# Attention scores of two mixers: full-precision products against three one-pass products of high and low parts

## The chip, the core and the metric

One core of one Trainium2 chip runs the whole kernel. The metric is device microseconds (us) of one execution. The engines meant below are TensorE (PE; PEld is its weight load), VectorE (DVE), ScalarE (ACT), GpSimd (POOL) and SyncE (SP), which only issues transfers.

## The reference

Two decoder layers over 512 tokens of width 2048. Layer 0 mixes an S5 state-space branch, eight forgetting-attention heads (FoX) and four memory heads. Layer 1 mixes eight latent-attention heads (MLA), eight sparse-attention heads (NSA, two key groups of four heads each) and four memory heads. The part that matters is the scores:

```
# FoX, per head: q, k (512, 128)
s = q @ k.T * scale + cum[:, None] - cum[None, :]        # causal, then softmax
# NSA, per head: three score sets from one q
s_c = q @ kc.T * scale + bias      # compressed keys, 31 of them (padded to 32)
s_s = q @ ks.T * scale + bias      # selected blocks; all of them here, so plain causal
s_w = q @ kw.T * scale + bias      # window of 512, causal here
o = g0 * softmax(s_c) @ vc + g1 * softmax(s_s) @ vs + g2 * softmax(s_w) @ vw
```

## The kernel before, in words

Every large product is made from split operands: a float32 value x is written as a high part (x rounded to the type float32r) and a low part (x minus the high part), and a product is the sum of three matmuls, high*high, high*low and low*high. The scores of FoX and NSA are not made so: their operands are plain float32, one matmul each, which the trace shows as two LDWEIGHTS and two MATMUL records.

The heads run in two sequences, `SEQ0` (FoX and memory heads of layer 0) and `SEQ1` (NSA and memory heads of layer 1). A sequence is a list of units, one unit being a score block of 128 query rows against `w` keys. For FoX a head has four units with `w` = 512, 128, 384, 256 (`ORDER` = 3, 0, 2, 1). For NSA a head has twelve: for each query block i, a unit of the selected keys, one of the window keys, both with `w` = (i+1)*128, and one of the 32 compressed keys; where i < 3 the first takes the compressed keys along in one matmul (`w` + 32 columns). `pe_seq` is written out by hand: step x makes the scores of unit x, the transposes of unit x-3 (L2609), the values of unit x-4 (L2620), and between them a slice of a large output projection, the fill (L283). DVE takes the maximum (L2702), ACT the exponential (L2664), DVE normalises (L2716, L2718), ACT copies the transposes out (L2656).

`pool_seq` on GpSimd issues the loads of the heads from its own queue, in program order: for head H it waits until the values of head H-2 are done and loads `v(H)`, then waits for the scores of head H-1 and loads q and k of head H+1 (`qk(H+1)`), then the gate of head H. For `SEQ1` the loads `qk(0)` are issued early, then GpSimd waits for the last MLA head (`MLA.fin`), and goes on with `v(0)`, `qk(1)`, `gate(0)`. A head's first score waits on the semaphore `a_ld` of its q and k loads, its first values on `a_vld`:

```python
if u["k"] == 0:
    pe.wait_ge(a_ld[u["r"]], t.ld0[0] + u["ld"])
```

Of the kernel before, what the change touches and what calls it, by code (L numbers as in the profile page):

```python
# [16 lines left out]
F32 = mybir.dt.float32  # L17
# [41 lines left out]
def build(nc, a):  # L59
    x, mem = a["x"][0], a["mem"][0]  # L60
    out = a["out"][0]
    with ExitStack() as ctx:
# [43 lines left out]
        bank_done = sem("bank_done")  # L106
        stored = sem("stored")
        ident_ok = sem("ident_ok")
        mask_ok = sem("mask_ok")
        gains_in = sem("gains_in")  # L110
        gains_pe, gains_ok = sem("gains_pe"), sem("gains_ok")
# [2621 lines left out]
        def pool_seq(pool, t, early=0):  # L2733

            def qk(H):
                if H >= 2:
                    pool.wait_ge(a_sc, t.u0 + t.end[H - 2])
                    if t.units[t.start[H - 2]]["bias"] is not None:
                        pool.wait_ge(a_mx, t.u0 + t.end[H - 2])
                t.units[t.start[H]]["load_qk"](pool, a_ld[H % 2])  # L2740

            def v(H):
                if H >= 2:
                    pool.wait_ge(a_pv, t.u0 + t.end[H - 2])
                t.units[t.start[H]]["load_v"](pool, a_vld[H % 2])

            def gate(H):
                if H >= 2:
                    pool.wait_ge(a_fin0, t.h0 + H - 1)
                pool.dma_start(t.units[t.start[H]]["out_gate"], t.units[t.start[H]]["gate_rows"]).then_inc(a_gl[H % 2], 16)  # L2750

            if early == 1:
                qk(0)
                return
            n = len(t.start)
            for H in range(n):
                if H == 0 and early == 0:
                    qk(0)
                if H == 0 and n > 1:
                    v(0)  # L2760
                    qk(1)
                    gate(0)
                    continue
                v(H)
                if H + 1 < n:
                    qk(H + 1)
                gate(H)

        resid_in = sem("resid_in")
        seqV = [s_tile(1024 * r, 2).rearrange("p (s j d) -> p s j d", s=2, j=4) for r in range(2)]  # L2770
# [5 lines left out]
        def head_units(H, units, **head):  # L2776
# [4 lines left out]
                out_.append(dict(u, H=H, r=H % 2, k=k, ld=ld, vld=vld, vn=head["vn"], **{n: head[n] for n in ("out_gate", "gate_rows", "load_qk", "load_v")}))  # L2781
            return out_

        def fox_head(h):

            r = h % 2
# [2 lines left out]
            def score(i):  # L2789
                def run(pe, bank):  # L2790
                    w = (i + 1) * P
                    nc.tensor.matmul(bank[:, 0:w], q[:, i * P:i * P + P], k[:, 0:w], start=True, stop=False)
                    return causal_mask(bank, w)
                return run

            def load_qk(pool, s_):
                qk = S[:, 8192 + 1536 * r:9216 + 1536 * r].rearrange("p (s t) -> p s t", s=2)
                pool.dma_start(qk, yE[2048:4096, :].rearrange("(s r) t -> r s t", s=2)[h * P:(h + 1) * P, :, :]).then_inc(s_, 16)
                pool.dma_start(cumB[r], cumD[h:h + 1, :].broadcast_to([P, T])).then_inc(s_, 16)

# [495 lines left out]
        def mla_score(i):  # L3296
            def score(pe, bank, r, b, x):
                w = (i + 1) * P
                q, k = MLA.inp[r][0], MLA.inp[r][1]
                nc.tensor.matmul(bank[:, 0:w], q[:, i * P:i * P + P], k[:, 0:w], start=True, stop=False)  # L3300
                if x % 4 == 0:
                    pe.wait_ge(rot_low, num(b, 2, x // 4 + 2 - 2 * MLA.b0))
                for part in range(2):
                    nc.tensor.matmul(bank[:, 0:w], rotQ[r][:, i * P:i * P + P], rotK[part][:, 0:w], start=False, stop=False)  # L3304
                causal_mask(bank, w).then_inc(MLA.sc, 1)
# [5 lines left out]
        qrS, krS = s_tile(10240), s_tile(11264)  # L3311

        rotQ, rotK = [A[:, 8 + e, :] for e in range(2)], [A[:, 10 + part, :] for part in range(2)]
        rot_high, rot_low = sem("rot_high"), sem("rot_low")

        def act_rot_keys(act):
            act.wait_ge(rope_ok, 2)
            nc.scalar.activation(rotK[0], krS, ACT.Copy).then_inc(rot_high, 1)

        def dve_rot_keys(dve):  # L3320
            dve.wait_ge(rot_high, 1)
            nc.vector.tensor_tensor(rotK[1], krS, rotK[0].bitcast(F32), ALU.subtract).then_inc(rot_low, 1)

        def act_rot(act, h):
# [7 lines left out]
        def dve_rot(dve, h):  # L3332

            half, other = [slice(64 * e, 64 * e + 64) for e in (h % 2, 1 - h % 2)]
            dve.wait_ge(rot_high, h + 2)
            nc.vector.tensor_tensor(rotQ[h % 2][other, :], qrS[half, :], rotQ[h % 2][half, :].bitcast(F32), ALU.subtract).then_inc(rot_low, 1)

        def rot_at(t, b, x):
# [58 lines left out]
        def pool_sum(pool, dst, e, h=0):  # L3397
            half = slice(64 * e, 64 * e + 64)
            if h >= 2:
                pool.wait_ge(rot_low, h)  # L3400
            nc.gpsimd.tensor_tensor(dst[half, :], qa[half, :], qb[half, :], ALU.add).then_inc(rope_ok, 1)

        def pool_rotary_load(pool, h):
# [19 lines left out]

        a_tiles = lambda k, n: A[:, k:k + n, :].rearrange("p k t -> p (k t)").bitcast(F32)
        nsaK0 = A[:, 16:20, :].rearrange("p k t -> p (k t)").bitcast(F32)
        nsaQ, nsaKw = [[nsaK0[:, o:o + 512], S[:, 8192 + o1:8704 + o1]] for o, o1 in ((0, 0), (1024 + NPAD, 512))]
        nsaKcs = [nsaK0[:, 512:1024 + NPAD], S[:, 10240:10752 + NPAD]]
        nsaKc, nsaKs = [[k[:, o:o + n] for k in nsaKcs] for o, n in ((0, NPAD), (NPAD, 512))]
        nsaB = [a_tiles(36, 3)[:, 0:LB], S[:, 13312:13312 + LB]]
        nsaVc = [a_tiles(39, 1)[:, 128:256], S[:, 15136:15264]]  # L3430
        nsaG = [S[:, 7680:8192], S[:, 9728:10240]]
# [1 line left out]
        def nsa_head(h):  # L3433

            r, grp = h % 2, h // 4
            keys = (nsaKs[r], nsaKw[r], nsaKc[r])

            def score(i, which, w):
                q = nsaQ[r][:, i * P:i * P + P]
                if i == 3:  # L3440
                    return lambda pe, bank: nc.tensor.matmul(bank[:, 0:w], q, keys[which][:, 0:w], start=True, stop=True)  # L3441
                if which == 0:
                    return lambda pe, bank: nc.tensor.matmul(bank[:, 0:NPAD + w], q, nsaKcs[r][:, 0:NPAD + w], start=True, stop=True)  # L3443
                if which == 1:
                    return lambda pe, bank: nc.tensor.matmul(bank[:, 0:w], q, nsaKw[r][:, 0:w], start=True, stop=True)  # L3445
                return None

            def load_qk(pool, s_):
                pool.dma_start(nsaQ[r], yO[1024 + h * P:1152 + h * P, :]).then_inc(s_, 16)
                for k in range(2):  # L3450
                    pool.dma_start((nsaKs, nsaKw)[k][r], yO[2560 + 256 * k + grp * P:2688 + 256 * k + grp * P, :]).then_inc(s_, 16)
                pool.dma_start(nsaB[r], biasD[:, h, :]).then_inc(s_, 16)
                if h == 0:
                    pool.wait_ge(cmp_out, 32)
                pool.dma_start(nsaKc[r], cmpD[grp, :, 0:NPAD]).then_inc(s_, 16)

            def load_v(pool, s_):
                pool.dma_start(nsaVc[r], cmpD[grp, :, NPAD:]).then_inc(s_, 16)
# [4 lines left out]
            for i in ORDER:  # L3463
                w = (i + 1) * P
                for which in (0, 1, 2):
# [4 lines left out]
                                      at=NPAD if which == 0 and i < 3 else 0,  # L3470
                                      v=(lambda j_, k=which: seqV[r][:, k, j_, :] if k < 2 else nsaVc[r]), bias=nsaB[r][:, o:o + n],
                                      gate=gtmS[:, i, col:col + 1], first=which == 0, last=which == 2))
            return head_units(h, units, ld=80 * (h // 2 + 1), vld=48 * (h // 2 + 1), vn=3, out_gate=nsaG[r],
                              gate_rows=yO[5120 + h * P:5248 + h * P, :], load_qk=load_qk, load_v=load_v)

        SEQ1 = Seq(1, [u for h in range(8) for u in nsa_head(h)] + [u for h in range(4) for u in mem_head(1, h, yO, 3584, 6144, 320, 192)], OUT1A, h1D, 1)

        def pe_nsa_gates(pe):
            pe.wait_ge(rope_in, 128)
# [467 lines left out]
```

## Time and profile before

| | us |
|---|---|
| median of 3 runs (lowest, highest) | 2172.55 (2171.39, 2172.58) |
| the profiled execution, its own time | 2172.06 |
| span of the profiled execution, first to last instruction | 2170.3 |

The rows further down are of the profiled execution. Times in them count from the span's first instruction. MATMUL records overlap: the duration of one holds its latency, so a spacing is read from start to start.

### The profile page before, as it was taken

The numbers are of one execution on the slowest core, as the hardware profiler recorded it, in microseconds if no ns is written. First come the engines' busy times: TensorE is split into PE (matmuls) and PEld (weight loads), VectorE is DVE, ScalarE is ACT, GpSimd is POOL, SyncE is SP. The second block draws the span as 40 slices with busy tenths as digits, with TensorE's granted clock in tenths as the row PEclk, the third lists the DMA queues.
The fourth block names the chain that finished last, engine by engine and source line by source line (L and its number), as shares of the span: only waits on it lengthen the run. The fifth ranks groups of instructions, "written<-read, shape, count | busy, mean of one in ns | idle before, by whom it ended". The sixth has DMA issues, their size and how long they took to land. (4 is left out here: it accounts for less than half of the span.)

```text
span 2170.3 us, 32485 instructions
## 1 busy us (share of the span) xinstructions
PE 2151.5 (99%) x12292; PEld 1810.8 (83%) x12292; DVE 1350.6 (62%) x2244; ACT 920.8 (42%) x1558; POOL 579.5 (27%) x771
## 2 busy tenths in 40 slices
PE   9999999999999999999999999999999999999998
PEld 8988888888888878888888899899886778788887
DVE  6632456655542237568649778877776648666876
ACT  6432333333332434434444444444433455555443
POOL 2626122223221002112001444444311255221120
PEclk9999999999999999999999999999999999999999
DMA  8645444444445436648644886878747966554674
GB/s 311 205 140 137 125 130 130 118 128 135 137 123 186 128 99 203 222 148 212 175 156 120 203 202 162 202 185 193 176 152 237 293 216 198 173 193 145 226 164 146
DMA packets 222423, 376.19 MB, mean 173 GB/s; under 512 B 22623, under 2 KB 102191, under 8 KB 220099
## 3 DMA queue, kind: packets, MB, share of 16 engines
q1 hardware_dynamic: 125152, 185.36, 27.8%
q0 software_dynamic: 63152, 126.20, 24.2%
q10 hardware_dynamic: 33971, 62.63, 7.9%
q8 instruction: 95, 1.56, 0.3%
q14 instruction: 53, 0.43, 0.1%
HBM read 310.30 MB, written 63.83 MB: 172 GB/s over the span
## 5 line engine op out<-in xcount | busy, mean ns | idle before, releaser
L283 PE MATMUL PS<-A,wsp 128*128 128x512 f32 (+2 forms) x3156 | 693.8, 379 | 2.9 <-issue 1.7
L283 PEld LDWEIGHTS PS<-A,wsp 128*128 128x128 f32 (+1 forms) x3156 | 564.2, 188 | 119.0 <-issue 9.1
L250 DVE TENSOR_TENSOR wsp<-wraw,wsp 128x1024 fp32r<-128x1024 f32 (+1 forms) x295 | 356.5, 1212 | 468.6 <-ACT wsp L243 467.0
L283 PE MATMUL PS<-wsp,A 128*128 128x512 f32 x2352 | 616.2, 403 | 0.0
L243 ACT ACTIVATE wsp<-wraw 128x1024 fp32r<-128x1024 f32 (+1 forms) x295 | 304.9, 1039 | 509.6 <-PE PS L283 406.7
L283 PEld LDWEIGHTS PS<-wsp,A 128*128 128x128 f32 x2352 | 423.8, 189 | 77.5 <-issue 4.8
L2044 PE MATMUL PS<-A,wsp 128*128 128x512 f32 x640 | 222.6, 397 | 0.0
L2046 PE MATMUL PS<-A,wsp 128*128 128x256 f32 x640 | 166.4, 280 | 0.0
L2001 DVE TENSOR_TENSOR wsp<-wraw,wsp 128x1024 fp32r<-128x1024 f32 x80 | 111.3, 1394 | 39.3 <-ACT wsp L1983 39.1
L2044 PEld LDWEIGHTS PS<-A,wsp 128*128 128x128 f32 x640 | 116.2, 188 | 21.8
L2046 PEld LDWEIGHTS PS<-A,wsp 128*128 128x128 f32 x640 | 120.7, 189 | 6.2
L1983 ACT ACTIVATE wsp<-wraw 128x1024 fp32r<-128x1024 f32 x80 | 84.8, 1060 | 95.0 <-PE PS L2046 49.0
L2656 ACT ACTIVATE S<-PS 128x256 f32<-128x256 f32 (+3 forms) x160 | 63.0, 394 | 131.8 <-PE PS L2609 131.0
L2057 PEld LDWEIGHTS PS<-S_rounded,wsp 128*128 128x128 f32 x960 | 117.8, 188 | 1.0
L2057 PE MATMUL PS<-S_rounded,wsp 128*128 128x256 f32 x960 | 118.3, 282 | 0.0
L1682 PE MATMUL PS<-wsp,A 128*128 128x512 f32 x504 | 114.9, 389 | 0.1
L1682 PEld LDWEIGHTS PS<-wsp,A 128*128 128x128 f32 x504 | 94.5, 188 | 20.1 <-DVE wsp L250 0.6
L1843 POOL TENSOR_TENSOR S<-wraw 128x1024 f32<-128x1024 f32 x20 | 59.3, 2967 | 189.3 <-DVE wsp L2001 76.7
L1983 ACT ACTIVATE wsp<-S 128x1024 fp32r<-128x1024 f32 x60 | 63.7, 1061 | 97.2 <-PE PS L2057 69.0
L2620 PEld LDWEIGHTS PS<-S 128*128 128x128 f32 x640 | 93.1, 191 | 9.4
L2001 DVE TENSOR_TENSOR wsp<-S,wsp 128x1024 fp32r<-128x1024 f32 x60 | 85.3, 1422 | 23.8 <-ACT wsp L1983 23.5
L2664 ACT ACTIVATE S<-PS,stats 128x256 f32<-128x256 f32 (+3 forms) x160 | 74.8, 467 | 51.4 <-DVE stats L2702 42.5
(455 smaller groups left out, 2841.4 us busy)
## 6 DMA issues: line engine op xcount, KB each, us to landing
wraw<-in_even_w_in_dram SPq DMA_DIRECT2D x112, 512.0 KB, 3.7
wraw<-in_odd_w_in_dram SPq DMA_DIRECT2D x96, 512.0 KB, 4.7
wraw<-in_w_out_dram SPq DMA_DIRECT2D x74, 512.0 KB, 4.6
wraw<-in_mem_w_kv_dram SPq DMA_DIRECT2D x32, 512.0 KB, 4.8
wraw<-in_w_out_dram POOLq DMA_DIRECT2D x24, 512.0 KB, 6.5
yO<-stage ACTq DMA_DIRECT2D x12, 1024.0 KB
yE<-stage ACTq DMA_DIRECT2D x10, 1024.0 KB
wraw<-in_odd_w_in_dram POOLq DMA_DIRECT2D x20, 512.0 KB, 8.8
```

What stands on the lines that cost most here:

```text
L243: nc.scalar.activation(wsp[:, q, 0, :, 0:j["cols"]], wraw[:, q, :, 0:j["cols"]], ACT.Copy).then_inc(w_hi, 1)
L250: nc.vector.tensor_tensor(wsp[:, q, 1, :, 0:j["cols"]], wraw[:, q, :, 0:j["cols"]], wsp[:, q, 0, :, 0:j["cols"]].bitcast(F32), ALU.subtrac ...
L283: mm = nc.tensor.matmul(dst, lhs, rhs, start=(s == 0 and kk == 0 and i == 0), stop=(s == j["spc"] - 1 and kk == 1 and i == 2))
L1682: mm = nc.tensor.matmul(PS[:, PAIR_BANK[product] + f, :], x_tile(j, product, 2 * s + kk, low)[:, f * P:f * P + P], wsp[:, q, wp, kk, :], s ...
L1983: nc.scalar.activation(fast_split(n % RAW, 0), fast_raw(FAST_RAW[product], s), ACT.Copy).then_inc(w_hi, 1)
L2001: nc.vector.tensor_tensor(fast_split(n % RAW, 1), fast_raw(FAST_RAW[product], s), fast_split(n % RAW, 0).bitcast(F32), ALU.subtract).then_ ...
L2044: mm = nc.tensor.matmul(dst, fast_split(q, 0)[:, w], fast_moving_both(product, 4 * s + kt), start=first, stop=last)
L2046: mm = nc.tensor.matmul(dst[:, 0:256], fast_split(q, 1)[:, w], fast_moving(product, 4 * s + kt, False), start=False, stop=False)
L2057: mm = nc.tensor.matmul(dst[:, f, :], w, fast_moving(product, 4 * s + kt, low), start=(s == 0 and f == 0 and m == 0), stop=(s == 1 and f = ...
L2620: mm = nc.tensor.matmul(PS[:, 7, i * P:i * P + P], u["v"](j_), seqT[x % 2][:, j_ * P:j_ * P + P], start=(j_ == 0 and u["first"]), stop=(j_ ...
L2656: nc.scalar.activation(seqT[x % 2][:, 0:n], PS[:, 6, 0:n], ACT.Copy).then_inc(a_ev, 1)
L2664: nc.scalar.activation(seqP[c][:, 0:w], PS[:, 4 + x % 2, u["at"]:u["at"] + w], ACT.Exp, bias=stats[:, 4 + c:5 + c], scale=-1.0 if u["bias" ...
```

## The change

For FoX and NSA the operands q and k are split into a high and a low part on GpSimd (`pool_split`: a copy to the high tile, a wait on GpSimd's own semaphore, and a subtraction in place that leaves the low part in the loaded tile). Each score matmul becomes three matmuls on float32r tiles. The split of head H+1 stands in GpSimd's program behind `gate(H)`; the split of NSA head 0 (both key tiles and q) stands behind `qk(0)`, ahead of the wait for `MLA.fin`; the keys of the second NSA group are split behind the split of head 3. A head's first score now also waits on `rot_low`. NSA keys are loaded once per group (with heads 0 and 2) instead of once per head. The semaphores `rot_high` and `rot_low`, which MLA uses, are shared, so MLA's counts are raised by a constant.

```diff
@@ -106,6 +106,8 @@
         bank_done = sem("bank_done")
         stored = sem("stored")
         ident_ok = sem("ident_ok")
+        rot_high, rot_low = sem("operand_high"), sem("operand_low")
+        FOX_SPLITS = 16
         mask_ok = sem("mask_ok")
         gains_in = sem("gains_in")
         gains_pe, gains_ok = sem("gains_pe"), sem("gains_ok")
...
@@ -2751,6 +2753,7 @@
             if early == 1:
                 qk(0)
+                pool_nsa_split(pool, 0)
                 return
             n = len(t.start)
             for H in range(n):
...
@@ -2760,11 +2763,18 @@
                     v(0)
                     qk(1)
                     gate(0)
+                    if t.l:
+                        pool_nsa_split(pool, 1)
+                    else:
+                        pool_fox_split(pool, 0)
+                        pool_fox_split(pool, 1)
                     continue
                 v(H)
                 if H + 1 < n:
                     qk(H + 1)
                 gate(H)
+                if H + 1 < 8:
+                    (pool_nsa_split if t.l else pool_fox_split)(pool, H + 1)
         resid_in = sem("resid_in")
         seqV = [s_tile(1024 * r, 2).rearrange("p (s j d) -> p s j d", s=2, j=4) for r in range(2)]
...
@@ -2781,6 +2791,19 @@
                 out_.append(dict(u, H=H, r=H % 2, k=k, ld=ld, vld=vld, vn=head["vn"], **{n: head[n] for n in ("out_gate", "gate_rows", "load_qk", "load_v")}))
             return out_
+        foxH = [[A[:, 16 + 2 * r + i, :] for i in range(2)] for r in range(2)]
+        def fox_operands(h):
+            o = 8192 + 1536 * (h % 2)
+            return [(S_rounded[:, o + 512 * i:o + 512 * i + 512], foxH[h % 2][i]) for i in range(2)]
+        def pool_fox_split(pool, h):
+            pool.wait_ge(a_ld[h % 2], 32 * (h // 2 + 1))
+            if h == 0:
+                pool.wait_ge(slot_used, E2["slot0"] + 1)
+            pool_split(pool, fox_operands(h), 2 * h)
         def fox_head(h):
             r = h % 2
...
@@ -2789,12 +2812,18 @@
             def score(i):
                 def run(pe, bank):
                     w = (i + 1) * P
-                    nc.tensor.matmul(bank[:, 0:w], q[:, i * P:i * P + P], k[:, 0:w], start=True, stop=False)
+                    (q_low, q_high), (k_low, k_high) = fox_operands(h)
+                    rows = slice(i * P, i * P + P)
+                    if i == ORDER[0]:
+                        pe.wait_ge(rot_low, 2 * h + 2)
+                    nc.tensor.matmul(bank[:, 0:w], q_high[:, rows], k_high[:, 0:w], start=True, stop=False)
+                    nc.tensor.matmul(bank[:, 0:w], q_low[:, rows], k_high[:, 0:w], start=False, stop=False)
+                    nc.tensor.matmul(bank[:, 0:w], q_high[:, rows], k_low[:, 0:w], start=False, stop=False)
                     return causal_mask(bank, w)
                 return run
             def load_qk(pool, s_):
-                qk = S[:, 8192 + 1536 * r:9216 + 1536 * r].rearrange("p (s t) -> p s t", s=2)
+                qk = S_rounded[:, 8192 + 1536 * r:9216 + 1536 * r].bitcast(F32).rearrange("p (s t) -> p s t", s=2)
                 pool.dma_start(qk, yE[2048:4096, :].rearrange("(s r) t -> r s t", s=2)[h * P:(h + 1) * P, :, :]).then_inc(s_, 16)
                 pool.dma_start(cumB[r], cumD[h:h + 1, :].broadcast_to([P, T])).then_inc(s_, 16)
...
@@ -3299,7 +3328,7 @@
                 q, k = MLA.inp[r][0], MLA.inp[r][1]
                 nc.tensor.matmul(bank[:, 0:w], q[:, i * P:i * P + P], k[:, 0:w], start=True, stop=False)
                 if x % 4 == 0:
-                    pe.wait_ge(rot_low, num(b, 2, x // 4 + 2 - 2 * MLA.b0))
+                    pe.wait_ge(rot_low, FOX_SPLITS + num(b, 2, x // 4 + 2 - 2 * MLA.b0))
                 for part in range(2):
                     nc.tensor.matmul(bank[:, 0:w], rotQ[r][:, i * P:i * P + P], rotK[part][:, 0:w], start=False, stop=False)
                 causal_mask(bank, w).then_inc(MLA.sc, 1)
...
@@ -3423,9 +3452,39 @@
         a_tiles = lambda k, n: A[:, k:k + n, :].rearrange("p k t -> p (k t)").bitcast(F32)
         nsaK0 = A[:, 16:20, :].rearrange("p k t -> p (k t)").bitcast(F32)
-        nsaQ, nsaKw = [[nsaK0[:, o:o + 512], S[:, 8192 + o1:8704 + o1]] for o, o1 in ((0, 0), (1024 + NPAD, 512))]
-        nsaKcs = [nsaK0[:, 512:1024 + NPAD], S[:, 10240:10752 + NPAD]]
-        nsaKc, nsaKs = [[k[:, o:o + n] for k in nsaKcs] for o, n in ((0, NPAD), (NPAD, 512))]
+        nsaQ = [A[:, 16, :], S_rounded[:, 8192:8704]]
+        nsaQh = [A[:, 15, :], A[:, 35, :]]
+        nsaK0r = A[:, 17:20, :].rearrange("p k t -> p (k t)")
+        nsaK0h = A[:, 32:35, :].rearrange("p k t -> p (k t)")
+        nsaKcs = [nsaK0r[:, 0:512 + NPAD], S_rounded[:, 10240:10752 + NPAD]]
+        nsaKcsH = [nsaK0h[:, 0:512 + NPAD], S_rounded[:, 15264:15776 + NPAD]]
+        nsaKw = [nsaK0r[:, 512 + NPAD:1024 + NPAD], S_rounded[:, 8704:9216]]
+        nsaKwH = [nsaK0h[:, 512 + NPAD:1024 + NPAD], S_rounded[:, 15776 + NPAD:16288 + NPAD]]
+        ROT_SPLITS = FOX_SPLITS + 9
+        def nsa_splits(h):
+            return ROT_SPLITS + h + 1 + 2 * (1 + (h >= 4))
+        def nsa_keys(grp):
+            return [(nsaKcs[grp], nsaKcsH[grp]), (nsaKw[grp], nsaKwH[grp])]
+        def pool_split(pool, operands, done):
+            for i, (whole, high_) in enumerate(operands):
+                nc.gpsimd.tensor_copy(high_, whole.bitcast(F32)).then_inc(rot_high, 1)
+                pool.wait_ge(rot_high, done + i + 1)
+                nc.gpsimd.tensor_tensor(whole, whole.bitcast(F32), high_.bitcast(F32), ALU.subtract).then_inc(rot_low, 1)
+        def pool_nsa_split(pool, h):
+            pool.wait_ge(a_ld[h % 2], SEQ1.ld0[0] + SEQ1.units[SEQ1.start[h]]["ld"])
+            if h == 0:
+                pool.wait_ge(rot_high, ROT_SPLITS)
+                pool_split(pool, nsa_keys(0), ROT_SPLITS)
+            pool_split(pool, [(nsaQ[h % 2], nsaQh[h % 2])], nsa_splits(h) - 1)
+            if h == 3:
+                pool_split(pool, nsa_keys(1), nsa_splits(3))
         nsaB = [a_tiles(36, 3)[:, 0:LB], S[:, 13312:13312 + LB]]
         nsaVc = [a_tiles(39, 1)[:, 128:256], S[:, 15136:15264]]
         nsaG = [S[:, 7680:8192], S[:, 9728:10240]]
...
@@ -3433,26 +3492,38 @@
         def nsa_head(h):
             r, grp = h % 2, h // 4
-            keys = (nsaKs[r], nsaKw[r], nsaKc[r])
+            def products(pe, bank, i, key, o, w):
+                if i == ORDER[0] and key == 0 and o <= NPAD:
+                    pe.wait_ge(rot_low, nsa_splits(h))
+                low, high_ = (nsaKcs, nsaKw)[key][grp], (nsaKcsH, nsaKwH)[key][grp]
+                rows = slice(i * P, i * P + P)
+                nc.tensor.matmul(bank[:, 0:w], nsaQh[r][:, rows], high_[:, o:o + w], start=True, stop=False)
+                nc.tensor.matmul(bank[:, 0:w], nsaQ[r][:, rows], high_[:, o:o + w], start=False, stop=False)
+                return nc.tensor.matmul(bank[:, 0:w], nsaQh[r][:, rows], low[:, o:o + w], start=False, stop=True)
             def score(i, which, w):
-                q = nsaQ[r][:, i * P:i * P + P]
                 if i == 3:
-                    return lambda pe, bank: nc.tensor.matmul(bank[:, 0:w], q, keys[which][:, 0:w], start=True, stop=True)
+                    return lambda pe, bank: products(pe, bank, i, which % 2, NPAD if which == 0 else 0, w)
                 if which == 0:
-                    return lambda pe, bank: nc.tensor.matmul(bank[:, 0:NPAD + w], q, nsaKcs[r][:, 0:NPAD + w], start=True, stop=True)
+                    return lambda pe, bank: products(pe, bank, i, 0, 0, NPAD + w)
                 if which == 1:
-                    return lambda pe, bank: nc.tensor.matmul(bank[:, 0:w], q, nsaKw[r][:, 0:w], start=True, stop=True)
+                    return lambda pe, bank: products(pe, bank, i, 1, 0, w)
                 return None
             def load_qk(pool, s_):
-                pool.dma_start(nsaQ[r], yO[1024 + h * P:1152 + h * P, :]).then_inc(s_, 16)
+                pool.dma_start(nsaQ[r].bitcast(F32), yO[1024 + h * P:1152 + h * P, :]).then_inc(s_, 16)
+                pool.dma_start(nsaB[r], biasD[:, h, :]).then_inc(s_, 16)
+                if h not in (0, 2):
+                    return
+                of = h // 2
                 for k in range(2):
-                    pool.dma_start((nsaKs, nsaKw)[k][r], yO[2560 + 256 * k + grp * P:2688 + 256 * k + grp * P, :]).then_inc(s_, 16)
-                pool.dma_start(nsaB[r], biasD[:, h, :]).then_inc(s_, 16)
+                    dst = (nsaKcs[of][:, NPAD:NPAD + 512], nsaKw[of])[k]
+                    pool.dma_start(dst.bitcast(F32), yO[2560 + 256 * k + of * P:2688 + 256 * k + of * P, :]).then_inc(s_, 16)
                 if h == 0:
                     pool.wait_ge(cmp_out, 32)
-                pool.dma_start(nsaKc[r], cmpD[grp, :, 0:NPAD]).then_inc(s_, 16)
+                pool.dma_start(nsaKcs[of][:, 0:NPAD].bitcast(F32), cmpD[of, :, 0:NPAD]).then_inc(s_, 16)
             def load_v(pool, s_):
                 pool.dma_start(nsaVc[r], cmpD[grp, :, NPAD:]).then_inc(s_, 16)
...
@@ -3470,10 +3541,10 @@
                                       at=NPAD if which == 0 and i < 3 else 0,
                                       v=(lambda j_, k=which: seqV[r][:, k, j_, :] if k < 2 else nsaVc[r]), bias=nsaB[r][:, o:o + n],
                                       gate=gtmS[:, i, col:col + 1], first=which == 0, last=which == 2))
-            return head_units(h, units, ld=80 * (h // 2 + 1), vld=48 * (h // 2 + 1), vn=3, out_gate=nsaG[r],
+            return head_units(h, units, ld=32 * (h // 2 + 1) + (0 if r else 48 * (1 + (h >= 2))), vld=48 * (h // 2 + 1), vn=3, out_gate=nsaG[r],
                               gate_rows=yO[5120 + h * P:5248 + h * P, :], load_qk=load_qk, load_v=load_v)
-        SEQ1 = Seq(1, [u for h in range(8) for u in nsa_head(h)] + [u for h in range(4) for u in mem_head(1, h, yO, 3584, 6144, 320, 192)], OUT1A, h1D, 1)
+        SEQ1 = Seq(1, [u for h in range(8) for u in nsa_head(h)] + [u for h in range(4) for u in mem_head(1, h, yO, 3584, 6144, (224, 128)[h % 2], 192)], OUT1A, h1D, 1)
         def pe_nsa_gates(pe):
             pe.wait_ge(rope_in, 128)
```

## Rows read from the trace of the kernel before

**Rows 1.** The page's line of busy time, TensorE.
```profile
PE 2151.5 (99%) x12292; PEld 1810.8 (83%) x12292; DVE 1350.6 (62%) x2244; ACT 920.8 (42%) x1558; POOL 579.5 (27%) x771
```

**Rows 2.** FoX and NSA stages: window; busy PE, PEld, DVE, ACT, POOL; clock; DMA share, GB/s.
```profile
828.00:920.00 92.00, 92.00 (x518) 76.29 (x517) 57.73 (x162) 40.35 (x101) 17.12 (x27) 1.00 0.62 204
1835.00:2002.00 167.00, 166.54 (x980) 135.50 (x980) 114.69 (x423) 91.31 (x292) 38.51 (x66) 1.00 0.55 184
```

**Rows 3.** Groups of instructions by line and shape, TensorE: score matmuls (count, busy, mean ns).
```profile
L2792 PE MATMUL PS<-S 128*128 128x512 f32 x16 | 8.2, 591 | 0.0
...
L2792 PE MATMUL PS<-S 128*128 128x128 f32 x16 | 3.1, 272 | 0.0
```

**Rows 4.** Timeline of TensorE at the first FoX score (start, length, group).
```profile
826.44 2.20 PE L283 MATMUL PS<-wsp,A 128*128 128x512 f32 x9
828.48 1.02 PE L2792 MATMUL PS<-S 128*128 128x512 f32 x2
...
830.14 0.38 PE L2792 MATMUL PS<-S 128*128 128x128 f32 x2
```

**Rows 5.** Timeline of TensorE, a run of float32r matmuls 256 wide.
```profile
1098.97 4.51 PE L774 MATMUL PS<-A,wsp 128*128 128x256 f32 x36
1103.32 0.93 PE L747 MATMUL PS<-ident,S 128*128 128x128 f32 x7
```

**Rows 6.** Timeline of TensorE's weight loads after a FoX score 128 wide.
```profile
830.25 0.19 PEld L2461 LDWEIGHTS PS<-masknegR,identR 128*128 128x128 f32 x1
830.36 0.30 PEld L283 LDWEIGHTS PS<-wsp,A 128*128 128x128 f32 x2
```

**Rows 7.** Timeline of TensorE's weight loads, an NSA score 32 wide.
```profile
1838.29 0.30 PEld L3441 LDWEIGHTS PS<-A 128*128 128x128 f32 x2 [0.43 <-ACT S L2664]
```

**Rows 8.** Timeline of GpSimd: loads for FoX head 3 (v of head 2 first).
```profile
848.09 0.76 POOL L2802 DMA_DIRECT2D S<-vE  x1 [10.31 <-PE PS L2620]
...
849.55 0.57 POOL L2799 DMA_DIRECT2D S<-cumD  x1
```

**Rows 9.** The cumD loads of all FoX heads, L2799.
```profile
L2799 POOL DMA_DIRECT2D S<-cumD x8: 569/569/574, 814.7 to 899.2; - x8
...
DMA to landing us min/median/max: 4.6/5.4/6.3
```

**Rows 10.** Timeline of TensorE: first scores of FoX heads 2 and 3.
```profile
848.56 1.02 PE L2792 MATMUL PS<-S 128*128 128x512 f32 x2
...
859.64 1.02 PE L2792 MATMUL PS<-S 128*128 128x512 f32 x2
```

**Rows 11.** NSA head 0: its last q and k load (L3455).
```profile
L3455 POOL DMA_DIRECT2D A<-cmpD x1: 545/545/545, 1823.9 to 1823.9; - x1
...
DMA to landing us min/median/max: 5.4/5.4/5.4
```

**Rows 12.** NSA head 0: its last two value loads (L3460).
```profile
L3460 POOL DMA_DIRECT2D S<-vO x2: 757/757/757, 1832.9 to 1833.7; - x2
...
DMA to landing us min/median/max: 4.3/5.1/5.8
```

**Rows 13.** Timeline of TensorE: first NSA score and first NSA values.
```profile
1835.50 1.02 PE L3441 MATMUL PS<-A 128*128 128x512 f32 x2
...
1841.72 0.49 PE L2620 MATMUL PS<-S 128*128 128x128 f32 x3
```

**Rows 14.** Groups of instructions by line and shape, GpSimd.
```profile
L1068 POOL TENSOR_SCALAR S<-S 128x512 f32<-128x512 f32 x1 | 1.5, 1507 | 0.1
...
L1078 POOL MEMSET S<- 128x512 f32 x1 | 0.5, 517 | 0.0
...
L2890 POOL CAST S<-ident 128x128 bf16<-128x128 f32 x1 | 0.3, 327 | 0.0
```

**Rows 15.** GpSimd's two-input products of 128 by 512, L3393 (min/median/max ns).
```profile
L3393 POOL TENSOR_TENSOR S<-S x5: 1271/1307/2089, 1727.8 to 1804.7; 128x512 f32<-128x512 f32 x5
```

**Rows 16.** Who waited for whom, weight loads in SEQ1 (us in total, times, longest).
```profile
PEld PS L2609 <- issue: 8.8, 34, 0.6
```

More of the change, by code:

```diff
@@ L3313, in build @@
         rotQ, rotK = [A[:, 8 + e, :] for e in range(2)], [A[:, 10 + part, :] for part in range(2)]
-        rot_high, rot_low = sem("rot_high"), sem("rot_low")
         def act_rot_keys(act):
@@ L3320, in dve_rot_keys @@
         def dve_rot_keys(dve):
-            dve.wait_ge(rot_high, 1)
+            dve.wait_ge(rot_high, FOX_SPLITS + 1)
             nc.vector.tensor_tensor(rotK[1], krS, rotK[0].bitcast(F32), ALU.subtract).then_inc(rot_low, 1)
@@ L3334, in dve_rot @@
             half, other = [slice(64 * e, 64 * e + 64) for e in (h % 2, 1 - h % 2)]
-            dve.wait_ge(rot_high, h + 2)
+            dve.wait_ge(rot_high, FOX_SPLITS + h + 2)
             nc.vector.tensor_tensor(rotQ[h % 2][other, :], qrS[half, :], rotQ[h % 2][half, :].bitcast(F32), ALU.subtract).then_inc(rot_low, 1)
@@ L3399, in pool_sum @@
             if h >= 2:
-                pool.wait_ge(rot_low, h)
+                pool.wait_ge(rot_low, FOX_SPLITS + h)
             nc.gpsimd.tensor_tensor(dst[half, :], qa[half, :], qb[half, :], ALU.add).then_inc(rope_ok, 1)
```

## The prediction

> **What bounds the kernel now.** Read the page's busy line first: TensorE is busy 99% of the span [rows 1]. As records overlap, that alone would not prove it, so the stages of the change come next. In the FoX stage TensorE covers all of 92.0 us and in the NSA stage 166.5 of 167.0, at granted clock 1.00 of 2.4 GHz, while DVE has 63% and 69% and GpSimd 19% and 23% [rows 2]. The time of these stages is TensorE's queue, matmul by matmul, so a change in spacing goes straight to the end unless something new makes TensorE wait. The reader is then to see spacings in the timelines, start to start, and what loads and waits on GpSimd stand ahead of the first score of a head. One warning sign is in the waits: in SEQ1 the weight load of a transpose was released late 34 times, 8.8 us in all [rows 16]; the array mostly still streamed then, but there is little slack behind DVE and ACT.
>
> **Part 1: the matmuls.** A float32 score of 512 columns is two records, .43 us apart (1.02 less the second's .59), so .86 us, in proportion to columns down to 128, where the two are .11 apart (.38 less .27) [rows 3, 4]. At 32 columns the two weight loads are still .11 apart (.30 less .19) [rows 7]: below 128 columns nothing gets cheaper.
>
> The new products are float32r. Nine fills of 512 columns take 2.04 us to the next start, .227 each [rows 4]; 36 of 256 columns take 4.35, .121 each [rows 5]. I take 288, 384 and 416 columns on the straight line between: .134, .174, .187. For narrow ones the nearest rows are the weight loads: that of the 128-column mask and the next lie .11 apart, and the next two again (.30 less .19) [rows 6], though 128 columns at the rate of 256 would stream in .06. So a product of 160, 128 or 32 columns costs .111, its weight load. The bounds: .111, and streaming alone (.075, .06, .015).
>
> A FoX head has widths 512, 384, 256, 128: before .86 + .64 + .43 + .22 = 2.15; after 3 x (.227 + .174 + .121 + .111) = 1.90. It saves .25, eight heads 2.0 us. The block of 128 gets dearer, .22 to .33.
> An NSA head has 512 twice, 416, 384, 288, 256, 160, 128 and 32: before 1.72 + .70 + .64 + .48 + .43 + .27 + .22 + .22 = 4.68; after 3 x (.454 + .187 + .174 + .134 + .121 + .111 + .111 + .111) = 4.21. It saves .47, eight heads 3.8 us.
> Together 5.8 us, and not the quarter that counting columns would give: with narrow products at streaming alone it would be 3 x (.05) more per FoX head and 3 x (.036 + .05 + .096) per NSA head, 5.6 in all, 11.4 us.
>
> The Trainium skill ("TensorE: Matmul & The Clock Gate", Back-to-back issue gap) gives some 81 ns per matmul in a stream of weight loads and matmuls at 128 columns. The trace's .11 for these tiles disagrees; by 81 ns the 32 narrow blocks would save 32 x 3 x .03 = 2.9 us more, 8.7 in all, an estimate from that page.
>
> **Part 2: the splits on GpSimd.** One split is a copy and a subtraction of 128 by 512. A two-input operation of this size takes 1.31 (least 1.27, most 2.09) [rows 15]. The copy isn't in the trace: its floor is a memset of that size, .52; a cast of a quarter of the columns takes .33, so four times that, 1.31, is too much by three fixed costs; a one-input operation with a constant took 1.51 [rows 14]. I take .9, between floor and cast; a pair is 2.2, with bounds 1.8 (.52 + 1.27) and 3.6 (1.51 + 2.09).
>
> FoX, from head 2 on, is a chain per head: values of head H-2 done, v, then q, k and cumD issued, landing, two pairs, first score. For head 3 cumD is issued at 849.55 [rows 8] and lands a median 5.4 later [rows 9], 854.95; two pairs end at 859.35. The score came at 859.64 [rows 10], and will want to come .25 earlier, 859.39. So it just fits: the cover is .04, and a pair over 2.25 makes TensorE wait twice the excess in a head with so short a slot (11.1 us between heads 2 and 3 [rows 10]). Cost 0 at 2.2; at 2.8, up to 6 heads x 1.1 = 6.6. Head 0 is safe: loaded from 814.7, landed 4.6 later [rows 9], two pairs to 823.7, score at 828.48 [rows 4]; v(1) and qk(2) queue behind the splits of heads 0 and 1, done near 828, and qk(2) waits for head 0's scores anyway.
>
> NSA head 0 is worse: three pairs, keys first. Its last load lands at 1823.9 + 5.4 = 1829.3 [rows 11]; three pairs and a sixteenth for the wider key tile, 6.7, end at 1836.0. The score came at 1835.50 [rows 13]: TensorE waits .5. Queued behind on GpSimd is v(0): the last vO was issued at 1833.7 and landed 5.8 later, 1839.5 [rows 12], for values at 1841.72 [rows 13]. Now the last vO goes at 1836.0 + .55 + .76 = 1837.3 and lands at 1843.1. So the values wait 1.4 in all, the .5 included; 0 at a pair of 1.8 (issue of the last vO at 1836.1, landing 1841.9), 3.2 at 2.8. Later NSA heads split one tile (head 3 three) in a slot of some 21 us (167 for eight) [rows 2]: nothing.
>
> **Part 3: the rest.** Fewer key loads: DMA was at .55 to .62 of its time [rows 2], gain nothing. The shared semaphores with raised counts, the wait for E2's slot and one more wait per head on TensorE: nothing, all long satisfied. DVE meets more GpSimd work; it is idle 37% in FoX and 31% in NSA [rows 2]. But with shorter scores the chain maximum, exponential, normalising, transpose comes due sooner. TensorE is nearest to waiting there [rows 16], so I take a quarter of NSA's 3.8 as given back, .9; bounds 0 and 3.8.
>
> **Sum.** -5.8 + 1.4 + .9 = -3.5 us on the profiled execution's 2172.06: 2168.6. The median of the runs stands .5 above it, so 2169.1, 0.16% faster. Within 0.2% (4.3 us) a measurement of this kernel can't tell a change.
>
> **Rivals.**
> *All of it is kept.* The copy is near the memset, a pair 1.9, and the transposes keep up: 5.8 to 6.1, 2166.5. For it: TensorE was never short of work. Against: the SEQ1 waits.
> *Columns decide.* Narrow products stream without paying their weight load: 11.4 us, 2161.2. Against: both weight-load rows.
> *Hand-offs take it back.* TensorE sits at the pace of DVE and ACT in SEQ1 and the whole 3.8 goes: 2172.55 - 2.0 + 1.4 = 2172.0.
> *GpSimd becomes the pace, slower.* A pair takes 3.0 (copy 1.51, subtraction 1.31, hand-offs between dependent instructions .2): six FoX heads wait up to 1.5 each, 9.0, NSA head 0 waits 3.8: -5.8 + .9 + 3.8 + 9.0 = +7.9, 2180.5. The gain is gone from a pair of 2.5 and the kernel slower by 0.2% from 2.8, were all slots that short. For it: a slot with a cover of .04, and the 2.09 of one product. Against: four of five products near 1.3 while DVE worked.
> The Trainium skill ("SBUF — State Buffer", Who interferes with whom) says that a VectorE instruction with two SBUF inputs and a GpSimd one that reads SBUF lock each other out for a whole instruction. The one product at 2.09 could be that; the median of 1.31 says it is rare. By the rule this rival gains.
>
> **How the numbers follow.** The forecast with losses of 1 to 4 us, .52 (of it .12 faster than 0.2%, .40 within); all kept .18; columns .05; hand-offs .11; GpSimd slower .14. So faster .12 + .18 + .05 = .35; same .40 + .11 = .51; slower .14. The range goes from all kept, 2166.0, to a pair of 2.8 in the heads with short slots, 2176.0, and leaves out columns and most of the slower rival.
>
> **What would show it.** Score products at .227 for 512 and .11 for 128 and 32 columns, start to start; GpSimd's copy at .9 and subtraction at 1.3; no gap of TensorE ahead of the 512-wide FoX scores; a gap of .5 ahead of the first NSA score and more ahead of its first values; more late releases of transposes. The prediction is wrong if the copy takes over 1.4, if narrow products come under .09, or if the gaps ahead of transposes grow past 2 us.

## The result, and the profile after

The changed kernel takes 2177.24 us (median of 13 runs, 2174.01 to 2178.83) against 2171.49 us for the kernel before beside it (13 runs): a ratio of 1.0025, 95% interval 1.0018 to 1.0033. It is slower by 5.75 us, where 3.5 us less were forecast, and lies above the forecast range (2166.0 to 2176.0). The profiled execution took 2174.57 us, span 2172.8, some 2.7 us under its own median. Lines of the changed kernel are two higher than before up to L2720; the FoX products stand on L2819 to L2821, the NSA products on L3502 to L3504, the GpSimd copy on L3474 and the subtraction on L3476.

First the two windows of [rows 2] and the 10 us after the first FoX scores (columns as there):

```profile
828.00:920.00 92.00, 88.71 (x523) 78.09 (x522) 67.12 (x164) 39.34 (x99) 45.04 (x54) 0.96 0.60 198
830.00:835.00 5.00, 1.71 (x8) 1.05 (x7) 4.20 (x13) 0.90 (x3) 0.42 (x1) 0.89 0.27 91
835.00:840.00 5.00, 5.00 (x16) 4.42 (x17) 1.67 (x7) 1.84 (x5) 0.00 (x0) 0.50 0.00 0
840.00:920.00 80.00, 80.00 (x490) 70.88 (x489) 59.25 (x145) 36.50 (x91) 42.70 (x51) 1.00 0.65 213
1835.00:2002.00 167.00, 163.61 (x1049) 143.87 (x1048) 125.46 (x423) 88.84 (x286) 57.92 (x75) 1.00 0.50 166
```

TensorE, which had no gap in the FoX stage, is idle 3.3 us of it, all between 830 and 835, and behind that wait the granted clock is 0.50 (1.2 of 2.4 GHz). From 840 on it is busy 80.00 of 80.00 us again. The NSA window lacks 3.4 us, against 0.5 before. The timeline of TensorE says where; first the FoX start, then the NSA start, to be read beside [rows 4, 13]:

```profile
829.47 0.27 PE L2820 MATMUL PS<-A,S_rounded 128*128 128x128 f32 x1
829.58 0.28 PE L2821 MATMUL PS<-S_rounded,A 128*128 128x128 f32 x1
829.69 0.27 PE L2463 MATMUL PS<-masknegR,identR 128*128 128x128 f32 x1
829.80 1.84 PE L285 MATMUL PS<-wsp,A 128*128 128x512 f32 x7
834.93 0.69 PE L2819 MATMUL PS<-A 128*128 128x384 f32 x1 [3.29 <-ACT S L2666]
...
1841.81 0.48 PE L3502 MATMUL PS<-A 128*128 128x512 f32 x1 [2.63 <-POOL A L3476]
...
1848.04 1.07 PE L2622 MATMUL PS<-S 128*128 128x128 f32 x8
```

The 128-wide products and the mask behind them start .11 apart, as forecast. Then TensorE waits 3.29 us for the exponential of unit 0 (L2666), and at NSA head 0 2.63 us for the last subtraction of the splits (L3476). The exponential is late because its maximum is: this is VectorE's timeline over the same time, of the kernel before

```profile
818.74 2.36 DVE L250 TENSOR_TENSOR wsp<-wraw,wsp 128x1024 fp32r<-128x1024 f32 x2
821.01 0.69 DVE L1501 TENSOR_TENSOR S<-S 128x512 f32<-128x512 f32 x1
821.73 0.43 DVE L1503 CAST A<-S 128x512 fp32r<-128x512 f32 x1
822.19 0.69 DVE L1505 TENSOR_TENSOR A<-S,A 128x512 fp32r<-128x512 f32 x1
...
828.21 0.07 DVE L2376 MEMSET stats<- 128x1 f32 x2
829.70 0.70 DVE L2702 CUSTOM_DVE_ANT_0 PS<-PS,S 128x512 f32<-128x512 f32 x1 [1.43 <-PE PS L2461]
```

and of the changed kernel, with GpSimd's timeline of its first pair (copy and subtraction) in a fence of its own:

```profile
818.17 2.77 DVE L252 TENSOR_TENSOR wsp<-wraw,wsp 128x1024 fp32r<-128x1024 f32 x2
820.86 1.78 DVE L1503 TENSOR_TENSOR S<-S 128x512 f32<-128x512 f32 x1
822.67 0.72 DVE L1505 CAST A<-S 128x512 fp32r<-128x512 f32 x1
823.42 1.66 DVE L1507 TENSOR_TENSOR A<-S,A 128x512 fp32r<-128x512 f32 x1
...
833.18 0.07 DVE L2378 MEMSET stats<- 128x1 f32 x2
833.31 0.70 DVE L2704 CUSTOM_DVE_ANT_0 PS<-PS,S 128x512 f32<-128x512 f32 x1
```

```profile
818.48 1.38 POOL L3474 CAST A<-S_rounded 128x512 fp32r<-128x512 f32 x1 [1.21 <-DMA S<-cumD]
819.94 2.14 POOL L3476 TENSOR_TENSOR S_rounded<-S_rounded,A 128x512 fp32r<-128x512 f32 x1
```

Before, VectorE worked off a chain without gaps ahead of the FoX heads (product, cast and subtraction per block of the GLU, and two weight splits) and then waited 1.43 us for the first score: that was its own slack. Behind it TensorE had some .83 more: the exponential of unit 0 was done at 831.27, the score that needs it came at 832.10. Now the same products take up to 1.78 instead of .69 us, the subtractions up to 1.66 instead of .69, and the chain from the weight splits to the memset takes 15.01 us (818.17 to 833.18) instead of 9.47. Of these 5.5 us more the two slacks cover 2.3, and TensorE waits the rest. GpSimd's instructions are longer there too, up to 1.38 for a copy and 2.14 for a subtraction, against these medians (min/median/max ns, the instructions of one line):

```profile
L3474 POOL CAST A<-S_rounded x20: 602/612/1532, 818.5 to 1969.4; 128x512 fp32r<-128x512 f32 x20
...
L3476 POOL TENSOR_TENSOR S_rounded<-S_rounded,A x20: 1272/1288/2328, 819.9 to 1970.3; 128x512 fp32r<-128x512 f32 x20
```

### The profile page after: what moved, and what is told of

The parts are those of the page before. It is cut to its first block and busy times, and to the rows that moved or that the text cites. A ratio compares the mean times of both kernels' runs of the same rounds, so it can differ in the third digit from the quotient of the medians.

```text
span 2172.8 us, 32717 instructions
## 1 busy us (share of the span) xinstructions
PE 2149.9 (99%) x12396; PEld 1824.5 (84%) x12396; DVE 1372.4 (63%) x2244; ACT 919.7 (42%) x1558; POOL 635.3 (29%) x809
## 5 line engine op out<-in xcount | busy, mean ns | idle before, releaser
L2666 ACT ACTIVATE S<-PS,stats 128x256 f32<-128x256 f32 (+3 forms) x160 | 74.7, 467 | 59.2 <-DVE stats L2704 50.4
```

The costliest lines, as they stand in the source:

```text
L2666: nc.scalar.activation(seqP[c][:, 0:w], PS[:, 4 + x % 2, u["at"]:u["at"] + w], ACT.Exp, bias=stats[:, 4 + c:5 + c], scale=-1.0 if u["bias" ...
```

## The experiments

**FoX heads 0 and 1 plain.** Kernel changed: the first two FoX heads are not split.

```diff
         def pool_fox_split(pool, h):
+            if h < 2:
+                return
...
+                    if h < 2:
+                        q_, k_ = [whole.bitcast(F32) for whole, _ in fox_operands(h)]
+                        nc.tensor.matmul(bank[:, 0:w], q_[:, i * P:i * P + P], k_[:, 0:w], start=True, stop=False)
+                        return causal_mask(bank, w)
```

> The changed kernel, but the scores of FoX heads 0 and 1 are made from plain float32 again, so that the first eight GpSimd instructions of the FoX stage are gone; heads 2 to 7 and NSA as changed. Theory (the splits at the stage's start hold up VectorE, the first maximum comes late and the clock falls after it): the first maximum comes near 829.7, no TensorE wait of 3.3 us at 834.9, no granted clock of 0.5 in 833 to 841, about 6 us less than the changed kernel, so near 2171. Rival (the splits of all heads are too much for GpSimd and VectorE): no more than the share of two heads in eight comes back, 1 to 2 us, near 2175.5.

Measured 2172.78 us (11 runs), 4.5 less than the changed kernel, where some 6 were expected; ratio to before 1.0003 (.9994 to 1.0012). VectorE waits for the score again, as before (its timeline), and the clock stays up (the window):

```profile
820.70 0.43 DVE L1505 CAST A<-S 128x512 fp32r<-128x512 f32 x1
828.67 0.70 DVE L2704 CUSTOM_DVE_ANT_0 PS<-PS,S 128x512 f32<-128x512 f32 x1 [1.43 <-PE PS L2463]
```

```profile
835.00:840.00 5.00, 5.00 (x30) 4.05 (x30) 3.68 (x10) 3.45 (x8) 1.75 (x3) 1.00 0.58 166
```

Two heads of eight give back most of the loss, so it is the stage's start and not GpSimd's pace in the heads. On the trace the start gives back all of its 6.0 us (14.28 to 8.29, table below), but from head 1 to the memory heads the stage takes 85.56 us instead of 84.49; .4 of that is a wait of head 2's first score for GpSimd's subtraction. In this execution TensorE still waits 2.76 us at the NSA start.

**NSA head 0 plain too.** The keys of group 0 are loaded whole into tiles of their own for head 0, and again, to be split, with head 1.

```diff
             def products(pe, bank, i, key, o, w):
+                if h == 0:
+                    k = (plainKcs, plainKw)[key]
+                    return nc.tensor.matmul(bank[:, 0:w], nsaQ[0].bitcast(F32)[:, i * P:i * P + P], k[:, o:o + w], start=True, stop=True)
```

> As the run before, and NSA head 0 plain float32 too: its keys are loaded whole into tiles of their own, and the first key group is loaded again and split with head 1. Theory (the loss is at the two starts alone): a further 2.4 us less (the wait of 2.6 us ahead of the first NSA score goes, .43 of saving of that head is lost), so near 2168 to 2169, 0.1 to 0.2% faster than the kernel before. Rival (the three pairs only move the contention to head 0's inside, where TensorE waits as long): near the run before, 2171.

Measured 2169.13 us: 3.65 less than the run before it, where 2.4 were expected, and ratio .9992 (.9983 to 1.0001). What the rest of the 3.65 is stays open; the profile of the run before has a fall of the clock near 1628 worth 1.7 us that this one has not (last section). The wait ahead of the first NSA score is gone, and inside head 0 the three pairs go nearly undisturbed (copies .64, .60 and .74, subtractions 1.34, 1.29 and 1.30) without a wait of TensorE: the contention didn't move in with them. With both starts plain the loss is gone: the two starts hold it.

**The same work in the kernel before.** Before, plus eight GpSimd instructions at the FoX start on spare tiles; nobody reads their results.

```diff
                     gate(0)
+                    if t.l == 0:
+                        extra_splits(pool)
...
+                    whole, high_, low = S[:, o:o + 512], A[:, 16 + 2 * i, :], A[:, 17 + 2 * i, :]
+                    nc.gpsimd.tensor_copy(high_, whole).then_inc(extra_done, 1)
...
+                    nc.gpsimd.tensor_tensor(low, whole, high_.bitcast(F32), ALU.subtract).then_inc(extra_done, 1)
```

> The kernel before, all products in plain float32, with the same eight copies and subtractions on GpSimd at the start of the FoX stage, on spare tiles, their results unused. Theory (GpSimd's instructions alone hold up VectorE, and TensorE waits for the first maximum): the first maximum comes 3 to 4 us later, the clock falls after the wait, 5 to 7 us slower than the kernel before, near 2177.5. Rival (the new products and TensorE's new waits do it): no change, within 1 us of the kernel before.

Measured 2177.20 us (7 runs), ratio 1.0028 (1.0017 to 1.0039). With plain float32 scores and no wait for splits on TensorE, the timelines of VectorE and TensorE show the same picture:

```profile
820.64 1.78 DVE L1501 TENSOR_TENSOR S<-S 128x512 f32<-128x512 f32 x1
822.46 0.72 DVE L1503 CAST A<-S 128x512 fp32r<-128x512 f32 x1
...
835.01 1.65 PE L2811 MATMUL PS<-S 128*128 128x384 f32 x2 [3.52 <-ACT S L2664]
```

The new products and waits of TensorE have no part in the FoX loss.

**TensorE kept busy in the gap.** Changed kernel, plus twelve unused matmuls.

```diff
                 seq_fill(pe, t, m0, m1)
+                if t.l == 0 and x == 2:
+                    for _ in range(12):
+                        nc.tensor.matmul(PS[:, 6, :], A[:, 0, 0:P], A[:, 1, :], start=True, stop=True)
```

> The changed kernel with twelve extra float32r matmuls 512 wide into an unused bank, behind the fill of step 2 of the FoX sequence, where TensorE waits for the first exponential; their results are unused. Theory (half of the loss at the FoX start is the clock that falls after the idle time): the 2.7 us that they take lie in the wait, the granted clock stays at 1.0 in 833 to 841, about 3 us less than the changed kernel, near 2174. Rival (the clock falls for another reason, or the idle time is not what sets it): the clock still falls, and the time is that of the changed kernel or up to 2.7 us more.

Measured 2173.08 us, 4.2 less than the changed kernel, where 3 were expected. More work on TensorE is faster (its timeline, and the window):

```profile
832.10 2.88 PE L2588 MATMUL PS<-A 128*128 128x512 f32 x12
835.59 0.44 PE L2822 MATMUL PS<-A 128*128 128x384 f32 x1 [0.61 <-ACT S L2669]
```

```profile
835.00:840.00 5.00, 4.41 (x25) 3.90 (x26) 3.21 (x11) 3.73 (x11) 0.63 (x1) 1.00 0.01 3
```

From the first score of FoX head 0 to that of head 1 it is 8.30 us before, 14.28 in the changed kernel and 11.67 here. So of the 6.0 us lost, 3.3 are the wait, and the other 2.6, which come back here, are the clock after it.

**Which instruction.** The same place in the kernel before, once with eight copies, once with eight subtractions (two SBUF inputs, results unused); one execution each. The edit of the copies against the run with extra work:

```diff
-                    nc.gpsimd.tensor_tensor(low, whole, high_.bitcast(F32), ALU.subtract).then_inc(extra_done, 1)
+                    nc.gpsimd.tensor_copy(high_, whole).then_inc(extra_done, 1)
```

> The kernel before with eight copies on GpSimd in place of the four copies and four subtractions that the run with extra work had (float32 to float32r, 128 by 512, results unused), at the start of the FoX stage. If VectorE is held up by any GpSimd instruction that reads and writes these memories, its instructions there take as much longer as in the run with copies and subtractions, up to the end of the copies, which comes earlier (8 at some .6 to 1.6 us). If the two-input subtraction is what holds it up, the slowest VectorE instructions stay under 1.2 times those of before, the first maximum comes within 1 us of 829.7, and TensorE does not wait. One look; the spans in the profile decide, the time within 2 us.

> The kernel before with eight two-input subtractions on GpSimd (128 by 512, results unused) at the start of the FoX stage. If any GpSimd instruction holds VectorE up, or the subtraction above all, VectorE is late by as much as with the mix or more (eight at some 1.3 to 2.1 us against four of them): the first maximum near 833 to 834 or later, TensorE waits 3 us or more, the time 5 to 8 us above the kernel before. If it is the copy, the first maximum comes within 1 us of 829.7.

VectorE with the copies, then with the subtractions:

```profile
820.33 1.10 DVE L1501 TENSOR_TENSOR S<-S 128x512 f32<-128x512 f32 x1
821.46 0.72 DVE L1503 CAST A<-S 128x512 fp32r<-128x512 f32 x1
822.22 0.98 DVE L1505 TENSOR_TENSOR A<-S,A 128x512 fp32r<-128x512 f32 x1
```

```profile
820.66 1.52 DVE L1501 TENSOR_TENSOR S<-S 128x512 f32<-128x512 f32 x1
822.22 1.41 DVE L1503 CAST A<-S 128x512 fp32r<-128x512 f32 x1
823.66 1.66 DVE L1505 TENSOR_TENSOR A<-S,A 128x512 fp32r<-128x512 f32 x1
```

| at the FoX start | weight splits to memset on VectorE | wait of TensorE | head 0 to head 1 |
|---|---|---|---|
| before | 9.47 | 0 | 8.30 |
| changed kernel: 4 copies, 4 subtractions | 15.01 | 3.29 | 14.28 |
| changed, heads 0 and 1 plain | 9.46 | 0 | 8.29 |
| before + 4 copies, 4 subtractions | 15.29 | 3.52 | 13.59 |
| before + 8 copies | 12.17 | 0.41 | 8.98 |
| before + 8 subtractions | 17.01 | 4.84 | 15.11 |

Neither case of the first expectation holds, and the second one's case "any instruction, or the subtraction above all" does (first maximum at 834.68, a wait of 4.84): both instructions hold VectorE up, a copy by (12.17 - 9.47) / 8 = .34 us, a subtraction by (17.01 - 9.47) / 8 = .94. Four of each make 5.1; 5.5 and 5.8 were measured. The 2.7 us of the copies go beyond VectorE's slack of 1.43, but with TensorE's .83 behind it only .4 of wait is left. No run has GpSimd instructions that only write, so whether reading alone does it is not shown. The times of the two executions (2177.05 and 2176.99 us, before 2171.80) say little, being one each: with the copies the granted clock also fell far from the edit. It is .83 on the mean of 1625 to 1635 and .51 on that of 1674 to 1681, 1.7 and 3.4 us of full clock.

**How much the rest is worth.** The kernel with both starts plain once more, and one in which no FoX head is split (the same test in the scores, and the semaphore counts to match).

```diff
-            if h < 2:
+            if h < 8:
                 return
...
-                    if h < 2:
+                    if h < 8:
```

> The kernel of the second run again (FoX heads 0 and 1 and NSA head 0 in plain float32, the others split), beside a kernel without any FoX split. By the spacings, six FoX heads save .25 each and seven NSA heads .43 each, 4.5 us in all: 2167 against the kernel before. Rival (something else of the change takes part of it back): near 2169.1, 2.4 us less than the kernel before, as the first time.

> All eight FoX heads in plain float32, as in the kernel before; NSA heads 1 to 7 split. If the six split FoX heads bring their 1.5 us, this one is 1.5 us slower than the run beside it, near 2170.6 if that one is at 2169.1. If GpSimd's work inside the FoX stage costs TensorE as much as the products save, the two are equal.

Measured 2168.63 us, ratio .9987 (.9978 to .9996), and 2168.39, ratio .9982 (.9972 to .9991). So with the starts left alone the change is a small gain, 2.9 and 3.1 us, less than the 4.5 that the spacings add up to. The traces show where these shrink: in the first kernel the FoX heads save 1.0 us (84.94 instead of 85.95 from head 1 to the memory heads) and the NSA heads 2.6 (167.16 instead of 169.71 from the first score to the memory heads), 3.6 in all. From the first score of FoX head 2 to that of head 7 the split heads take 60.11 us (847.93 to 908.04), the plain ones 61.00 (847.58 to 908.58), .18 a head; in the medians they save nothing. Both fit intervals of about 2 us either way, so what the FoX splits are worth stays open; NSA heads 1 to 7 carry the gain (167.14 without any FoX split).

## Why the prediction was wrong

**Part 1 held.** From head 1 to the memory heads the FoX stage is shorter by 1.46 us over seven heads, .21 each (.25 forecast); the NSA heads by .43 each (.47). Narrow products cost .11, so *Columns decide* is out. *All of it is kept* met its conditions in the heads, yet with both starts plain the kernel stands at 2168.6 to 2169.1 and not at 2166.5.

**Part 2, the duration, held on the safe side.** Undisturbed a copy takes .61 (.9 forecast) and a subtraction 1.29, with .08 between them (the .2 in the slower rival was in no row): a pair takes 1.97 instead of 2.2. Beside VectorE's work three of the twelve FoX pairs from head 2 on took 2.8 to 3.0. No FoX score from head 2 on waits, though: TensorE is busy 80.00 of 80.00 us. *GpSimd becomes the pace* did not happen in the heads. That the cover is thin was right (by the rows a pair of 2.22 uses it up, not 2.25): the wait of .4 in the run with heads 0 and 1 plain shows it.

**Part 2, "Head 0 is safe", is the step that failed,** together with Part 3's "DVE meets more GpSimd work", costed at nothing. I checked whether GpSimd would be done by 828.48 and found 4.8 us of cover; the splits of head 0 were in fact done in time (the first score came at 827.91). What I did not look at is who else works in those 10 us: VectorE, without a gap, with 1.43 us of slack before the first maximum. Its idle share of 37% [rows 2] says nothing of that stretch: that window begins at 828.00, where the chain ends. The eight instructions cost VectorE 5.5 us, and so TensorE 3.3 of wait and 2.6 of clock: 6.0 us at a place forecast at 0.

The slower rival carried the right mechanism, in its last paragraph, and the wrong place. The lock that the Trainium skill states ("SBUF — State Buffer", Who interferes with whom: a VectorE instruction with two SBUF inputs, or a copy or cast in a two-port mode, and a GpSimd one that reads SBUF keep each other out for a whole instruction) was put aside because GpSimd's products had a median of 1.31 [rows 15]. The runs agree with the rule: a product of two SBUF tiles goes from .69 to up to 1.78, a cast from .43 to up to 1.41, and both engines are slowed. They agree on what was not slowed, too: at the NSA start four VectorE memsets, the first two beside a subtraction of GpSimd, take 2.11 us, as before without one.

The trace of before already had it, for a reader of VectorE's rows beside GpSimd's; first the two engines near 1791, then near 1742:

```profile
1791.59 1.34 POOL L3394 TENSOR_TENSOR S<-S 128x512 f32<-128x512 f32 x1
1791.90 1.30 DVE L2335 CAST A<-S 128x512 fp32r<-128x512 f32 x1
...
1742.40 1.23 DVE L250 TENSOR_TENSOR wsp<-wraw,wsp 128x1024 fp32r<-128x1024 f32 x1 [6.62 <-ACT wsp L243]
1742.68 2.09 POOL L3393 TENSOR_TENSOR S<-S 128x512 f32<-128x512 f32 x1
```

A cast of VectorE that takes .42 elsewhere (at 1827.59) took 1.30 when it began inside a GpSimd product, and GpSimd's product kept its 1.3. The one product of 2.09 is the only one of the five of [rows 15] that began well inside a VectorE product of two SBUF tiles. So the median of GpSimd said which engine waited, not that the lock is rare.

**Part 2, NSA head 0, was mis-sized.** The wait is 2.63 us instead of .5. The three pairs took 8.3 instead of 6.7 us (1833.39 to 1841.67), by the traces for the same reason: VectorE's last MLA cast and subtraction and its weight splits run beside them, and two weight splits take 3.85 instead of 2.36:

```profile
1833.39 0.64 POOL L3474 CAST A<-A 128x544 fp32r<-128x544 f32 x1 [5.20 <-DMA A<-cmpD]
...
1837.86 1.60 POOL L3474 CAST A<-A 128x512 fp32r<-128x512 f32 x1
1839.55 2.12 POOL L3476 TENSOR_TENSOR A<-A 128x512 fp32r<-128x512 f32 x1
...
1836.69 3.85 DVE L252 TENSOR_TENSOR wsp<-wraw,wsp 128x1024 fp32r<-128x1024 f32 x2
1840.60 2.11 DVE L3985 MEMSET S<- 128x512 f32 x4
```

Some .3 of the rest is the last key load, which was issued that much later against the score than before. The granted clock stays at 1.00 behind this wait (1836 to 1860). The second wait, for v(0), didn't come: its last load was issued at 1842.91 and landed in 5.0 us, at 1847.91, just ahead of the first values at 1848.04.

**Part 3, the hand-offs, went the other way.** The row that the .9 rests on was misread: [rows 16] puts the 8.8 us in 34 places down to "issue", time in which the profile shows nothing that was waited for, and not to VectorE or ScalarE (to VectorE it puts 1.4 us in 6 places). Over the same part of SEQ1 the changed kernel has

```profile
PEld PS L2611 <- issue: 1.5, 5, 0.7
```

and .7 us in one place put down to VectorE. So nothing shows the .9 as lost, and *Hand-offs take it back* is out.

**The sum, on the trace.** +6.0 (FoX start) + 2.6 (NSA start) - 1.5 (FoX heads 1 to 7) - 3.4 (NSA) = +3.7; the span grew by 2.5, and the missing 1.2 lie in stages that the change doesn't touch, .6 of it before the FoX stage. One of these stages holds, in this execution, a fall of the clock worth 1.7 us (last section). The medians grew by 5.75. Why the other executions of the changed kernel are slower than the profiled one is not settled: their granted clocks over the whole span, .996 to .998, lie around its .997, so a longer fall of the clock at the FoX start explains little of it.

## What to carry to other kernels

An off-path engine that is idle on average can still be the wrong place for work: ask not only when the moved work must be done, but whose instructions run beside it, whether the two engines hold each other up, and how much slack there is in that stretch, not over the stage. Read the rows of both engines for that: the one that waits may be the other one. Here GpSimd splits of the same size made no FoX score wait from head 2 on, and cost TensorE 6.0 us where they ran beside a dense VectorE chain; leaving three heads of sixteen alone turned a loss of 5.75 us into a gain of 2.4 and 2.9 in two measurements. A stall of TensorE can cost more than itself: at the FoX start waits of 3.29, 3.52 and 4.84 us cost 6.0, 5.3 and 6.8 with the clock that fell behind them, while that of 2.63 at the NSA start cost no clock.

## What the runs showed that was not expected

The granted clock does not fall after every wait of the same kind. Near 1628 TensorE has waits of 1.5 to 1.9 us in the kernel before and in all the others. In the profiled execution of before the clock stays at 1.00 behind them; with the extra copies, where those waits are much the same, it does not (columns as in [rows 2], before first, then before with eight copies):

```profile
1625.00:1630.00 5.00, 3.14 (x43) 2.14 (x42) 5.00 (x20) 0.69 (x4) 0.00 (x0) 1.00 0.09 14
1630.00:1635.00 5.00, 5.00 (x48) 3.97 (x50) 2.98 (x12) 0.42 (x2) 0.00 (x0) 1.00 0.28 58
```

```profile
1625.00:1630.00 5.00, 2.99 (x42) 1.97 (x41) 5.00 (x20) 0.69 (x4) 0.00 (x0) 0.97 0.04 7
1630.00:1635.00 5.00, 5.00 (x17) 3.98 (x16) 3.24 (x13) 0.35 (x1) 0.00 (x0) 0.69 0.30 65
```

By the mean clocks (.97 and .69 over 5 us each) such a fall is worth 1.7 us. It is in the profiled executions of the changed kernel and of five of the eight edited ones, three of them with the plain float32 scores of before, and in none of the other four: the kernels of the first two runs are the same up to there, and one has it and the other has not, so the edits don't decide it. It may be a part of what single executions of one kernel differ by: of the 21 executions of before beside the last two runs, the four of 2175 us and more have a granted clock of .996 or .997 over the span, the others .998 or .999.
